# Two weights of the entry split on other engines, sums of RWKV taken from rounded parts, and splits and copies moved at the borders of a decoder step

## The reference: one step of a two-layer hybrid decoder

```python
kk = kk / jnp.maximum(jnp.sqrt(jnp.sum(kk * kk, -1, keepdims=True)), 1e-12)        # "ss"
var = jnp.mean(jnp.square(y - mean), -1, keepdims=True)                           # "var"
bonus = jnp.sum(r_h * k_h * r_k.astype(f32), -1, keepdims=True) * v_h              # "bo"
```

## Time and profile before

| | |
|---|---|
| time, median of 3 runs | 3319.75 us (3316.57 to 3322.81) |
| the profiled execution's own time | 3316.99 us |
| its span in the trace | 3315.2 us |
| mean granted TensorE clock | 0.983 of full speed |
| busy PE / DVE / ACT / POOL | 3178.5 / 2171.6 / 1171.5 / 1089.3 us |
| one pair of RWKV | 122.6 to 129.0 us |
| transfers | 322.71 MB, mean 97 GB/s |

### The profile page before, as it was taken

How to read it: one execution, slowest core, us unless ns; L and a number is a source line. 1 busy time by engine, 2 the same in 40 slices (tenths; PEclk the granted TensorE clock), 3 DMA queues, 4 the chain that set the end, 5 groups by cost and what they waited for, 6 DMA issues and landing times. The chain is left out here.

```text
span 3315.2 us, 74986 instructions
## 1 busy us (share of the span) xinstructions
PE 3178.5 (96%) x31728; PEld 3007.5 (91%) x31728; DVE 2171.6 (66%) x3016; ACT 1171.5 (35%) x2377; POOL 1089.3 (33%) x630
## 2 busy tenths in 40 slices
PE   7999889999999989999999999999998999999998
PEld 6999768888888879999999999999997999999998
DVE  5112774665666658666788884566546976668888
ACT  3344222332332434444433352221212444443334
POOL 3322110110114013444455533222202354445543
PEclk9999889999999999999999999999998999999999
DMA  5113540100101112444544411111113144455442
GB/s 167 65 59 103 184 134 9 33 30 9 37 30 53 59 35 74 147 142 141 199 143 143 143 59 58 60 66 60 59 53 117 49 146 143 143 192 169 143 143 92
DMA packets 151200, 322.71 MB, mean 97 GB/s; under 512 B 16904, under 2 KB 50356, under 8 KB 150744
## 3 DMA queue, kind: packets, MB, share of 16 engines
q1 hardware_dynamic: 106480, 242.53, 22.4%
q10 hardware_dynamic: 44392, 75.42, 6.7%
HBM read 227.12 MB, written 93.12 MB: 97 GB/s over the span
## 5 line engine op out<-in xcount | busy, mean ns | idle before, releaser
L247 PE MATMUL psum<-act_hi,w_hi 128*128 128x352 f32 x2088 | 704.7, 338 | 25.1 <-issue 7.3
L247 PE MATMUL psum<-act_hi,w_lo 128*128 128x352 f32 x2088 | 677.6, 325 | 0.0
L247 PE MATMUL psum<-act_lo,w_hi 128*128 128x352 f32 x2088 | 676.6, 324 | 0.0
L232 POOL TENSOR_TENSOR w_hi<-w_raw,derived 128x1024 fp32r<-128x1024 f32 x83 | 163.1, 1965 | 1421.8 <-PE psum L247 1342.9
L247 PEld LDWEIGHTS psum<-act_hi,w_hi 128*128 128x128 f32 x2088 | 397.4, 190 | 54.0 <-issue 23.1
L247 PEld LDWEIGHTS psum<-act_lo,w_hi 128*128 128x128 f32 x2088 | 398.6, 191 | 2.5 <-issue 0.2
L247 PEld LDWEIGHTS psum<-act_hi,w_lo 128*128 128x128 f32 x2088 | 397.8, 190 | 0.0
L1064 PE MATMUL psum<-ff_near,ff_w_hi 128*128 128x264 f32 x2048 | 379.5, 286 | 4.3 <-issue 1.5
L1064 PEld LDWEIGHTS psum<-ff_near,ff_w_hi 128*128 128x128 f32 x2048 | 317.5, 188 | 10.2 <-issue 9.6
L1064 PE MATMUL psum<-ff_far,ff_w_hi 128*128 128x264 f32 x1536 | 286.2, 287 | 8.9 <-ACT ff_b L1196 6.7
L1064 PE MATMUL psum<-ff_near,ff_w_lo 128*128 128x264 f32 x1024 | 291.1, 284 | 0.0
(11 more groups left out here) (565 smaller groups left out, 7370.7 us busy)
## 6 DMA issues: line engine op xcount, KB each, us to landing
ff_du_raw<-u SPq DMA_DIRECT2D x224, 264.0 KB, 2.8
w_raw<-weights SPq DMA_DIRECT2D x84, 512.0 KB, 3.3
u<-ff_stage SPq DMA_DIRECT2D x128, 264.0 KB, 2.3
ff_raw<-mlp SPq DMA_DIRECT2D x64, 512.0 KB, 3.9
u<-ff_side SPq DMA_DIRECT2D x96, 264.0 KB, 3.7
s_cache<-cache_a ACTq DMA_DIRECT2D x32, 512.0 KB, 7.1
ff_dt<-mlp SPq DMA_DIRECT2D x64, 256.0 KB, 4.5
ff_dt<-mlp SPq DMA_DIRECT2D x32, 512.0 KB, 7.2
```

The lines of the kernel that those rows point to most:

```text
L232: pool.tensor_tensor(hi, raw, self.zeros, ALU.add).then_inc(s.sem, s.step())
L247: last = pe.matmul(out, w[:, k, :], h[:, k, cols], start=(start and k == ks[0] and m == 0), stop=(stop and k == ks[-1] and m == 2))
```

## The change

It has five parts.

1. Entry: weights 1 and 2 are rounded on ACT (`act_split`) and DVE subtracts (`dve_split`); POOL only counts the steps. The six loads of constants go behind the norm's third part on ACT's queue.
2. RWKV: `ss`, `bo` and, for all pairs but the last, `var` are no longer f32 matmuls. ACT copies the summed tile into fp32r (`sum_high`), DVE subtracts the rest into a low part (`low_part`), and PE does two fp32r matmuls for each piece of columns (`split_sums`). The last pair's `var` and all `mean` sums stay f32. Unit (0, 2) comes ahead of `var` and `ss` on PE, and its copy on ACT ahead of the norm's steps.
3. POOL in RWKV: the splits of weights 0 and 1 of a later pair also wait for a point of the second half (`quiet`), and the output projection's rows follow behind the same points.
4. MLP: for w = 1 ACT copies `ff_b` ahead of `square_out` "11", and `ff_c` ahead of two weight roundings.
5. HGRN: DVE, ahead of its last adds, makes the low parts of the first four weights. Slots rotate from head to head (`ORDERS`), so that those for the output projection come free with n = 0, 1, 2 of the last head, and its early groups stand at m = 2, 3, 5.

```diff
+    def act_split(self, act, n):
+        s = self.plan.steps["act"]
+        act.wait_ge(self.sem("w_loaded"), (n + 1) * 16)
+        act.activation(self.slots[n][0].rearrange("p k c -> p (k c)"), self.w_raw[:, :], ACT.Copy)\
+            .then_inc(s.sem, s.step(f"act.weight{n}"))
+    def dve_split(self, dve, n):
+        s = self.plan.steps["dve"]
+        hi, lo = (w.rearrange("p k c -> p (k c)") for w in self.slots[n])
+        dve.wait_ge(*self.plan.at(f"act.weight{n}"))
+        dve.tensor_tensor(lo, self.w_raw[:, :], hi.bitcast(F32), ALU.subtract).then_inc(s.sem, s.step(f"dve.weight{n}"))
...
         for w in range(TILES_A):
+            if w in (1, 2):
+                pool.wait_ge(*K.plan.at(f"dve.weight{w}"))
+                pool.sem_inc(s.sem, s.step() + s.step())
+                continue
...
+        def split_sums(i, name, high, low):
+            for c in range(NT):
+                cols, out = slice(c * TC, (c + 1) * TC), ps[:, B.of(f"{i}.{name}{c}"), 0:TC]
+                pe.wait_ge(*B.emptied(f"{i}.{name}{c}"))
+                pe.wait_ge(*at(f"dve.B.{i}.{name}_low"))
+                pe.matmul(out, K.half_ones_r[:, :], high[:, cols], start=True, stop=False)
+                pe.matmul(out, K.half_ones_r[:, :], low[:, cols], start=False, stop=True)\
+                    .then_inc(s.sem, s.step(f"pe.B.{i}.{name}{c}"))
...
+            unit(i + 1, 0, 2)
             if i:
-                sums(i - 1, "var", self.rs, f"act.B.{i - 1}.sq" + ("" if live else "{c}"))
-            if not live:
-                break
-            sums(i, "ss", self.e[4], f"act.B.{i}.kk2")
-            unit(i + 1, 0, 2)
+                split_sums(i - 1, "var", self.sum_high[0], self.rs_low)
+            split_sums(i, "ss", self.sum_high[1], self.e4_low)
...
-            sums(i, "bo", raw[1], f"dve.B.{i}.rk")
+            split_sums(i, "bo", self.sum_high[0], self.raw_low[i % 2])
...
             evacuate(i + 1, 1, 1)
+            act.wait_ge(*at(f"dve.B.{i}.rk"))
+            act.activation(self.sum_high[0][:, :], raw[1][:, 0:T], ACT.Copy).then_inc(s.sem, s.step(f"act.B.{i}.bo_high"))
...
+            def low_part(owner, name, dst, src, high):
+                dve.wait_ge(*at(f"act.B.{owner}.{name}_high"))
+                dve.tensor_tensor(dst[:, :], src, high[:, :].bitcast(F32), ALU.subtract)\
+                    .then_inc(s.sem, s.step(f"dve.B.{owner}.{name}_low"))
...
+                if i >= 2 and n < 2:
+                    pool.wait_ge(*K.plan.at(self.quiet(i - 2, n)))
                 K.split_weight(pool, self.w0 + 3 * i + n, n)
+    def quiet(self, i, n):
+        return f"dve.B.{i}." + ("YX32_0w0", "S3")[n]
...
+            if w == 1:
+                keep_both(w, 1)
+                self.square_out(act, w, "11")
+                keep_both(w, 2)
+                for p in (6, 7):
+                    self.weight_high(act, w + 1, p)
...
+    ORDERS = ((3, 2, 1, 0), (2, 3, 1, 0), (2, 1, 3, 0), (1, 2, 3, 0), (1, 2, 0, 3), (1, 0, 2, 3), (0, 1, 2, 3), (0, 1, 2, 3))
     def slot(self, h, n):
-        return (3, 2, 1, 0)[n]
+        return self.ORDERS[h][n]
...
-                if 3 <= m < 6:
+                if m in (2, 3, 5):
...
-            out0.pool(pool, [f"pe.B.5.in{j}.{NT - 1}" for j in range(3)])
+            out0.pool(pool, [rwkv.quiet(rwkv.PAIRS - 2, 0), rwkv.quiet(rwkv.PAIRS - 2, 1), f"pe.B.5.in2.{NT - 1}"])
...
-            out1.pool(pool, [f"pe.C.{KC - 1}.in{n}.{NT - 1}" for n in (3, 2, 1)])
+            out1.pool(pool, [hgrn.slot_freed(KC - 1, slot) for slot in range(3)])
...
-            setup.act_masks(act, K)
             norm_mix0.act_second(act)
             attention.bias_store(act)
             norm_mix0.act_third(act)
+            setup.act_masks(act, K)
```

More of the change, by code:

```diff
@@ L1269, in act @@
                 self.weight_high(act, w + 1, p)
-            self.square_out(act, w, "11")
-            keep_both(w, 1)
-            for p in (6, 7):
-                self.weight_high(act, w + 1, p)
-            keep_both(w, 2)
+            if w == 1:
[4 more added lines that the diff above has]
+                    self.weight_high(act, w + 1, p)
+            else:
+                self.square_out(act, w, "11")
+                keep_both(w, 1)
+                for p in (6, 7):
+                    self.weight_high(act, w + 1, p)
+                keep_both(w, 2)
             self.weight_high(act, w + 1, 5)
@@ L1543, in dve @@
                     self.row_sum(dve, g, q)
+        if self.following is not None:
+            self.following.dve_weights(dve)
         for u in range(16):
@@ L1582, in dve_masks @@
         dve.wait_ge(K.sem("constants_loaded"), 6 * 16)
+        dve.tensor_tensor(K.half_ones_r[:, :], K.half_ones[:, :], K.derived[:, 1:2].broadcast_to([P, P]), ALU.add)\
+            .then_inc(K.plan.steps["dve"].sem, K.plan.steps["dve"].step())
         dve.tensor_copy(K.masks[:], K.masks_in[:]).then_inc(s.sem, s.step("dve.setup.masks"))
@@ L2419, in __init__ @@
         self.e = [take(f"e{n}", [P, T]) for n in range(5)]
+        self.L = take("L", [P, 2, 4, 64])
+        high_at = a
         self.YX = take("YX", [P, 2, 2, 4, 64])
-        self.L, self.T1, self.LZ = (take(n, [P, 2, 4, 64]) for n in ("L", "T1", "LZ"))
+        self.T1, self.LZ = (take(n, [P, 2, 4, 64]) for n in ("T1", "LZ"))
+        self.sYX = take("sYX", [NS, 2, 2, NS])
+        self.sum_high = [K.at(f"b_sum_high{n}", [P, T], F32R, high_at + n * WIDE) for n in range(2)]
+        assert high_at + 2 * WIDE <= a
         self.KA, self.RB, self.RK = (take(n, [P, 2, 4, P]) for n in ("KA", "RB", "RK"))
+        rs_at = a
         self.rs = K.at("b_rs", [P, T], F32, a)
@@ L2617, in pe @@
             unit(i + 1, 0, 1)
+            if not live:
+                sums(i - 1, "var", self.rs, f"act.B.{i - 1}.sq{{c}}")
+                break
+            unit(i + 1, 0, 2)
             if i:
-                sums(i - 1, "var", self.rs, f"act.B.{i - 1}.sq" + ("" if live else "{c}"))
-            if not live:
-                break
-            sums(i, "ss", self.e[4], f"act.B.{i}.kk2")
-            unit(i + 1, 0, 2)
+                split_sums(i - 1, "var", self.sum_high[0], self.rs_low)
+            split_sums(i, "ss", self.sum_high[1], self.e4_low)
             unit(i + 1, 1, 0)
@@ L3315, in dve @@
                 self.shifted(dve, i, 1)
+                if i:
+                    low_part(i - 1, "var", self.rs_low, self.rs[:], self.sum_high[0])
                 dve.wait_ge(*at(f"act.B.{i}.w2"))
@@ L3777, in act_weights, with dve_weights @@
                 .then_inc(s.sem, s.step(f"act.C.weight{n}"))
+    def dve_weights(self, dve):
+        s = self.K.plan.steps["dve"]
+        for n in range(4):
+            hi, lo = (flat(t) for t in self.K.slots[self.slot(0, n)])
+            dve.wait_ge(*self.K.plan.at(f"act.C.weight{n}"))
+            dve.tensor_tensor(lo, self.first_raw[n][:, :], hi.bitcast(F32), ALU.subtract).then_inc(s.sem, s.step(f"dve.C.weight{n}"))
     def out_rows(self, h, out):
@@ L4160, in pool @@
         for n in range(4):
-            hi, lo = (flat(t) for t in K.slots[self.slot(0, n)])
-            pool.wait_ge(*K.plan.at(f"act.C.weight{n}"))
-            pool.tensor_tensor(lo, self.first_raw[n][:, :], hi.bitcast(F32), ALU.subtract).then_inc(s.sem, s.step() + s.step())
+            pool.wait_ge(*K.plan.at(f"dve.C.weight{n}"))
+            pool.sem_inc(s.sem, s.step() + s.step())
         for h in range(1, self.HEADS):
             for n in range(4):
-                pool.wait_ge(*K.plan.at(f"pe.C.{h - 1}.in{n}.{NT - 1}"))
+                pool.wait_ge(*K.plan.at(self.slot_freed(h - 1, self.slot(h, n))))
                 K.split_weight(pool, self.w0 + 4 * h + n, self.slot(h, n))
```

25 lines of the change are left out of this document (22 added, 3 removed).

## The result

The changed kernel took 3293.67 us (median of 4 runs, 3289.85 to 3297.53) beside 3318.16 (4 runs) of the kernel before: a ratio of 0.9926, 95% interval 0.9905 to 0.9946, 24.5 us faster. The forecast was 3283 in 3260 to 3305: right in direction and range, with 36.5 us of gain forecast where 24.5 came. What follows is mostly about the 12 us between.

A forecast was written before the change was run, and what follows sets the result against it. PE, busy 96% of the span, was taken as the bound, so gains come from less PE work or closed gaps and their lower clock. Terms summed to 36.5 us, giving 3283 us, range 3260 to 3305.

The forecast's parts named there:

- The rounded sums in pairs 1 to 4: RWKV: cheaper sums save PE 2.46 us a pair, less a 0.35 wait, with DVE freed of POOL's blocking; 8.4 us gained.
- Rival D: RWKV sums: two rounded matmuls cost what one f32 does, so most groups save nothing; 3293 us, chance 0.07.
- A: Rival in RWKV: POOL's blocking of DVE isn't relieved and DVE sets every pair's turn; slower, 3329 us, chance 0.07.
- The second halves: RWKV behind each turn: no term except pair 4, where later row splits stop slowing DVE; 5.5 us gained (0 to 5.9).
- rival B: RWKV: POOL's blocking only moves to second halves, 2.1 us in each of four pairs; 3300 us, chance 0.18.
- Pair 5: Last RWKV pair: no POOL work to be freed of, so DVE's subtractions delay the turn; 4 us lost (0 to 6).
- Pair 0: First RWKV pair: the 3.04 us wait for ACT's copy goes, with clock loss and cheaper sums; 6.5 us gained.
- Entry: Entry: splits off POOL unblock DVE's adds, and ACT's constant loads move later; 4.5 us gained (2 to 6.2).
- MLP: Both MLPs, w = 1: PE's 3.4 us wait for `ff_b` goes, 1.4 left to late rounded weights; 3.8 us gained each.
- MLP 0 to HGRN: Border before HGRN: DVE makes low parts itself, removing PE's wait for `ff_du_last_lo`; 1.5 us gained (-2.8 to 2.2).
- the rotation: HGRN: rotating slots change when POOL splits in each head, where PE has no gap to lose; 0.5 us lost.
- End of HGRN: Last head: second output projection weight split earlier, so PE's 7.3 us wait goes; 7 us gained (4 to 13).

The follow-up runs named there:

- no_quiet: Changed kernel with POOL's splits in RWKV and of the output projection's rows released as before the change, rounded sums kept; 3334.0 us, ratio 1.0046 to before.
- all_f32: Changed kernel with ss, bo and var as f32 matmuls again, POOL's moved splits kept; 3294.8 us, ratio 0.9929 to before.
- after_again: The changed kernel run once more, unaltered, for a second profile; 3292.6 us, ratio 0.9923 to before.
- early_345: Changed kernel with the output projection's three early groups back at m = 3, 4, 5 of the last head, rotated slots kept; 3290.2 us.
- mlp_old: Changed kernel with ACT's old order in both MLPs at w = 1; 3295.9 us.
- masks_back: Changed kernel with the entry's six loads of constants back in the middle of ACT's queue; second sum of squares on PE at 46.4 us, no total time given.
- last_f32v: Changed kernel with f32 sums in pair 5's first half (ss and bo of pair 5, var of pair 4); 3289.2 us, ratio 0.9908 to before.

## Why the prediction was right, and where it failed

**The rounded sums in pairs 1 to 4: right.** 2.46 us less PE work a pair were forecast with a wait of 0.35; the turn came 2.4 earlier, and no row shows a wait of PE before it. That is 9.7 us for four pairs where 8.4 was forecast. (The group at 718.41 that gave the price is the sum `mean` and not `var`, as the earlier trace rows calls it; it has the same shape.) That DVE had to be freed of 7.35 us for it is shown by no_quiet, where it wasn't and the turn went from 42.8 to 49.5. The prediction counted this as cover, not as gain, and all_f32 confirms that for first halves the cover alone is worth nothing. Rival D (two rounded matmuls as dear as one f32) is excluded by the 0.97 us of a group. A holds as a mechanism but did not occur. Its price was too low: 5.05 us for each of pairs 0 to 4, where the turns of no_quiet came 6.6 to 6.8 later than before in pairs 1 to 4. I added DVE's 3.75 less its idle time; the 2.2 us wait for ACT's copies was not in it.

**The second halves: the step that failed most.** The prediction let them stay and took 5.5 off pair 4's. From the start of pair 0 to the turn of pair 5, before took 657.8 us in both profiles. Forecast were 16.4 less (8.4 + 6.5 + 5.5 - 4); the five profiles with the changed RWKV (changed, after_again, early_345, mlp_old, masks_back) took 644.0 to 651.5, 9.9 less in the mean. First halves of pairs 1 to 4 gave 9.7 of it, pair 0's turn 5.1 in the mean of both (38.3 against 45.3 and 41.5), and pair 5 cost 3.8 (2.6 to 4.5). The second halves were 1.1 longer, where 5.5 were to go.

Of that, pair 4 gave 2.7 in the mean (83.9 against 86.6), up to 5 in single profiles, so its term was twice what came. The mechanism was right: by the rows, DVE's instructions beside POOL took 6.6 and 6.7 us more than the same ones elsewhere in pair 4's second half before, and 1.5 to 2.5 after.

Pairs 1 to 3 together took 246.4 against 241.4. That is 1.7 each, over the 1 us that the prediction gave as the sign of rival B. B's mechanism isn't there, though. POOL is now busy 12.7 us in such a second half instead of 4.3, yet no DVE instruction beside it in pairs 0 to 3 took over 0.25 us more than the same one elsewhere. And no_quiet, without the moved splits, has 246.4 as well, as has all_f32, with them and without rounded sums. Most of the 5.0 us is half clock: 3.4 us lost to it in both profiles before, 5.1 to 10.2 in the five, 7.5 in the mean. Why the clock fell more often is open. It differs from one execution to the next by as much (239 to 251 us in versions of one PE queue here), and two profiles of the kernel before are too few to say what belongs to the change.

**Behind the turn of pair 5: a loss without a term.** From there to the first product of MLP 0, before took 161.2 us in both profiles and the changed kernel 163.6 and 162.3 (161.6 to 165.7 in its versions). PE's waits there are the same, 11.0 to 11.5 us; the granted clock is 0.960 and 0.968 instead of 0.979.

**Pair 5: right.** Forecast -4, its turn came 2.6 to 4.5 us later. The way was the forecast one: no POOL to be freed of, so the subtractions went straight onto the limiting queue. last_f32v gave most of it back (34.2; the 0.6 us over the 33.6 of before is what the term had for POOL's splits of the rows).

**Pair 0: half right.** 6.5 forecast; 7.1 against the first profile, 3.2 against the second, in which the wait for the copy was 0.8 us instead of 3.0 from the start. I had read a term from one execution that another didn't have.

**Entry: right, 4.5 forecast and 4.7 measured** up to the first transposition of the attention, with the adds at 4.30 us instead of 7.94 and the split ahead of them at 1.22:

```profile
23.91 1.22 DVE L249 TENSOR_TENSOR w_lo<-w_raw,w_hi 128x1024 fp32r<-128x1024 f32 x1
25.04 4.30 DVE L350 TENSOR_TENSOR nm_acc<-nm_acc,nm_sq 128x352 f32<-128x352 f32 x7
```

Up to pair 0 another 2.3 us came in the mean that no term had; it wasn't looked into.

**MLP: the mechanism right, the size wrong in MLP 1.** Forecast 3.8 in each. MLP 0 became 3.3 us shorter and MLP 1 1.1, in the means of the two profiles of each kernel. The wait for `ff_b` went whole, and the waits that came for it are 1.9 us in MLP 0 and 2.3 and 3.1 in MLP 1, where 1.4 was left to them. The step that failed is "late next are the rounded weights, 1.4": late next was DVE's chain through `ff_r`, which ACT's square and with it PE's banks wait for, in both MLPs. The earlier trace rows showed it: a square that waited 5.12 us for DVE. What moved in the queue was ACT's copy; the square still waited 4.2 us for DVE.

**MLP 0 to HGRN: half; the rotation: right.** 1.5 forecast, 0.8 came from the last weight's products to the first head (81.2 to 80.4). The waits for `ff_du_last_lo` (2.8 in all) went, but PE then waited for DVE's last adds, 4.4 us where it had waited 1.0 before:

```profile
PE psum L413 <- DVE nm_acc L350: 4.4, 1, 4.4
```

That fits the risk which the range named, DVE's 5.0 us ahead of these adds not being covered. The rotation: -0.5 forecast, -0.5 came.

**End of HGRN: half.** Forecast 7, 3.2 came (the last head at 66.3 and 66.0 us before, 63.2 and 62.6 now). That the weights would be ready was right, and I named the rows' transfer as what could be late, but on `c_ks`. It ended the wait of the early group itself, which the new order had put in front; early_345 was 2.4 to 3.5 us faster, of the 3.8 that were missing.

In sum, from the means of two profiles of each kernel (us gained):

| stretch | forecast | measured |
|---|---|---|
| to the attention's first transposition | 4.5 | 4.7 |
| from there to pair 0 | 0 | 2.3 |
| pair 0 to the turn of pair 5 | 16.4 | 9.4 |
| from there to MLP 0 | 0 | -1.7 |
| MLP 0 up to `ff_du_first` | 3.8 | 3.3 |
| from there to the first head of HGRN | 1.5 | 0.3 |
| HGRN | 6.5 | 2.8 |
| MLP 1 up to `ff_du_first` | 3.8 | 1.1 |
| the rest | 0 | 0.5 |
| sum | 36.5 | 22.7 |

The range held because the misses stayed inside it, not because the terms were right: RWKV and what follows it fell 8.7 short, and luck up to pair 0 gave 2.3. That gaps come back under another releaser stood only in the prediction's last sentence, at up to 15 us. The MLPs, the stretch before HGRN and its end showed it. The clock in the second halves of pairs 1 to 3 and behind pair 5 was in no term.

## What to carry to other kernels

Price an edit at its position in the queue. Here work added to DVE beside PE was free only as long as POOL didn't hold it, and the test for that was one run with the cover taken away. When a wait is removed, the next late releaser is often in the same row of the trace (what the engine that ended the wait had itself been waiting for), so cost the removal at the difference between the two. Read terms of 2 to 5 us from two profiles of each kernel: here one execution's stretches at half clock moved three second halves by up to 10 us. And compare lengths between the same instructions, not only the waits: in MLP 0 the waits fell by 1.5 us and the stretch by 3.3.
